# Differential attention: 768 columns scaled by ScalarE, and the products with the value in four portions of two key blocks

## What is computed

```python
sc = jnp.einsum('bqhmd,bkhmd->bmhqk', qb, k) * scale + bias[None, None]
p = jax.nn.softmax(sc, axis=-1)
a = p[:, 0] - lam * p[:, 1]
return jnp.einsum('bhqk,bkhd->bqhd', a.astype(v.dtype), v)
```

## Time and profile before

| | |
|---|---|
| median of 3 runs | 4118.57 us (4106.49 to 4128.41) |
| the profiled execution | 4106.46 us, of which its span 4104.7 us |
| busy over the span | PE 3779.6 us (92%), POOL 2494.2 (61%), DVE 2231.6 (54%), ACT 1659.1 (40%) |
| mean granted clock of PE | 0.979 of 2.4 GHz |

### The profile page before, as it was taken

The page is one execution under the profiler, slowest core; times in us unless marked ns, Lnnn a source line. Parts: engine busy times, 40 slices in busy tenths (PEclk is TensorE's granted clock), DMA queues, the critical chain, the costliest instruction groups (busy, mean ns, idle before and its releaser), DMA issues. The chain is left out here.

```text
span 4104.7 us, 51191 instructions
## 1 busy us (share of the span) xinstructions
PE 3779.6 (92%) x19002; PEld 2621.1 (64%) x19002; DVE 2231.6 (54%) x3655; ACT 1659.1 (40%) x2882; POOL 2494.2 (61%) x1393
## 2 busy tenths in 40 slices
PE   8999999999989999789989999999999898997898
PEld 8788774455545666557777897755455455665587
DVE  3012125555569999675531021255555699996754
ACT  3112104333348888661031121033333588886610
POOL 1221326877769999754512213277777699997555
PEclk9999999999999999999989999999999999999999
DMA  5333534232420222235354335322234202223353
GB/s 177 128 134 116 166 117 107 57 81 54 107 56 1 56 56 52 66 99 187 128 172 133 128 120 159 124 54 54 55 67 94 56 1 56 56 52 86 87 184 129
DMA packets 179678, 391.37 MB, mean 95 GB/s; under 512 B 17854, under 2 KB 98984, under 8 KB 167784
## 3 DMA queue, kind: packets, MB, share of 16 engines
q1 hardware_dynamic: 178568, 386.70, 33.6%
q10 hardware_dynamic: 864, 1.41, 0.2%
HBM read 254.88 MB, written 135.67 MB: 95 GB/s over the span
## 5 line engine op out<-in xcount | busy, mean ns | idle before, releaser
L1279 POOL TENSOR_TENSOR mla_sum_pool<-mla_sum_pool,mla_probs 128x1024 f32<-128x1024 f32 (+1 forms) x336 | 783.4, 2332 | 231.3 <-ACT mla_probs L1240 206.6
L1297 DVE TENSOR_REDUCE carry_row_max<-psum 128x1 f32<-128x512 f32 x688 | 473.4, 691 | 447.4 <-PE psum L1112 441.8
L1240 ACT ACTIVATE mla_probs<-psum 128x1024 f32<-128x1024 f32 x384 | 373.3, 1021 | 721.2 <-PE psum L1149 716.6
L1539 ACT ACTIVATE diff_probs<-psum,diff_shift 128x1024 f32<-128x1024 f32 x512 | 566.6, 1112 | 194.6 <-DVE diff_shift L1614 188.7
L1607 DVE TENSOR_REDUCE diff_row_max<-psum 128x1 f32<-128x1024 f32 x512 | 612.7, 1219 | 52.0 <-PE psum L1474 39.0
L1486 PE MATMUL psum<-ident,diff_probs 128*128 128x128 f32 x2048 | 329.4, 283 | 107.5 <-DVE diff_turned L1641 72.5
L624 PE MATMUL psum<-in_x_hi,in_w_hi 128*128 128x512 f32 x1024 | 403.1, 394 | 2.7 <-ACT in_mla_val L733 2.7
L624 PE MATMUL psum<-carry_firsts,in_w_hi 128*128 128x512 f32 x1024 | 403.4, 394 | 0.0
L624 PE MATMUL psum<-in_x_hi,in_w_lo 128*128 128x512 f32 x1024 | 400.3, 391 | 0.0
L1486 PEld LDWEIGHTS psum<-ident,diff_probs 128*128 128x128 f32 x2048 | 215.5, 141 | 286.0 <-issue 187.5
L1162 PE MATMUL psum<-mla_probs,mla_v_op 128*64 128x512 f32 x1536 | 373.2, 607 | 0.0
(11 more groups left out here) (206 smaller groups left out, 7383.9 us busy)
## 6 DMA issues: line engine op xcount, KB each, us to landing
in_w_raw<-in_w_in SPq DMA_DIRECT2D x64, 512.0 KB, 3.9
split_d<-in_out SPq DMA_DIRECT2D x64, 512.0 KB, 2.6
raw_d<-in_out SPq DMA_DIRECT2D x32, 512.0 KB, 2.6
mq_d<-in_out SPq DMA_DIRECT2D x48, 256.0 KB, 3.4
mk_d<-in_out SPq DMA_DIRECT2D x48, 256.0 KB, 3.9
carry_firsts<-split_d SPq DMA_DIRECT2D x48, 256.0 KB, 7.9
carry_weights<-split_d SPq DMA_DIRECT2D x48, 256.0 KB, 7.7
carry_weights<-split_d SPq DMA_DIRECT2D x16, 768.0 KB, 17.6
```

Source lines behind the costliest of these rows:

```text
L1240: nc.scalar.activation(probs[:, s % RING, :].rearrange("p (a n) -> p a n", n=CH), psum[:, S0 + 2 * (s % 2):S0 + 2 * (s % 2) + 2, :], ACT.E ...
L1279: nc.gpsimd.tensor_tensor(acc, start, probs[:, s % RING, mine], ALU.add).then_inc(pool_added, 1)
L1297: nc.vector.tensor_reduce(row_max[:, u % 2, qb, n:n + 1], psum[:, sweep_bank(g), :], AX.X, ALU.max).then_inc(maxed, 1)
L1539: nc.scalar.activation(dst[:, half * HALF:(half + 1) * HALF].rearrange("p (a n) -> p a n", n=CH), banks(n, m, half), ACT.Exp, bias=shift[: ...
```

## The change

Two things are changed in `diff_attention`, for both layers.

The split of the scaling: ACT's `scale` takes columns 0 to 767 instead of 0 to 511, and POOL's first instruction 768 to 1023 instead of 512 to 1023.

The order on PE: an iteration becomes four equal quarters of one half of scores, one batch of transposes, and one portion of products. A portion is two key blocks instead of four, there are four portions in an iteration instead of two, and each stands behind a batch of transposes instead of in front of one. The scores and the batches keep their order among themselves. What each portion waits for (`copied`, `o_ready`) names the same units as before. The queues of DVE, ACT and SP keep their order.

```diff
+    SCALED = 6 * P
...
-                    b, chunk = g // (NB // 2) % 2, 2 * ((n - 4) % 2) + place
-                    if chunk == 0 and g >= 1:
+                    b, first = g // (NB // 2) % 2, 8 * ((n - 4) % 2) + 2 * place
+                    if first == 0 and g >= 1:
                         pe.wait_ge(o_ready, g)
-                    pe.wait_ge(copied, 4 * (2 * g + 1) + chunk + 1)
-                    for kb in range(4 * chunk, 4 * chunk + 4):
+                    pe.wait_ge(copied, 4 * (2 * g + 1) + first // 4 + 1)
+                    for kb in range(first, first + 2):
...
-                    if chunk == 3:
+                    if first == NB - 2:
                         last.then_inc(pv_done, 1)
...
                 for n in range(UNITS + DRAIN + 2):
                     on = n < UNITS
-                    if on:
-                        scores(n, 0, 0)
-                    turns(n - LAG - 1, 3)
-                    if on:
-                        scores(n, 0, 1)
-                    products(n, 0)
-                    turns(n - LAG, 0)
-                    if on:
-                        scores(n, 1, 0)
-                    turns(n - LAG, 1)
-                    if on:
-                        scores(n, 1, 1)
-                    products(n, 1)
-                    turns(n - LAG, 2)
+                    for half in range(4):
+                        if on:
+                            scores(n, half // 2, half % 2)
+                        turns(n - LAG - (half == 0), (half - 1) % 4)
+                        products(n, half)
...
-                    first = probs1[:, n % DEEP1, 0:CH]
+                    first = probs1[:, n % DEEP1, 0:SCALED]
...
-                    second, third = probs1[:, n % DEEP1, CH:HALF], probs1[:, n % DEEP1, HALF:SEQ]
-                    nc.gpsimd.tensor_tensor(second, second, ratio[:, n % 2:n % 2 + 1].broadcast_to([P, HALF - CH]),
+                    second, third = probs1[:, n % DEEP1, SCALED:HALF], probs1[:, n % DEEP1, HALF:SEQ]
+                    nc.gpsimd.tensor_tensor(second, second, ratio[:, n % 2:n % 2 + 1].broadcast_to([P, HALF - SCALED]),
                                             ALU.mult).then_inc(times_ratio, 1)
```

## The result

| | before | after |
|---|---|---|
| median | 4116.33 us (4 runs, 4106.49 to 4128.41) | 4258.02 us (4 runs, 4244.85 to 4259.80) |
| ratio | | 1.0345, 95% interval 1.0327 to 1.0363 |
| span of the profiled execution | 4104.7 us | 4257.0 us |
| busy over the span | PE 3779.6, POOL 2494.2, DVE 2231.6, ACT 1659.1 | PE 3903.4, POOL 2438.1, DVE 2225.2, ACT 1686.5 |
| mean granted clock of PE | 0.979 | 0.976 |

The account below looks back on a forecast made before the run. POOL at 7.835 us a unit and a loop around PE were taken as nearly equal bounds. Portions lengthen units to 8.76 (upper) and 8.335 (lower), mean 8.55; 0.715 more over 120 units is 85.5 us, forecast 4204, range 4154 to 4240.

Parts of the forecast that it names:

- The two bounds on top of each other: In the differential stage, POOL at 7.835 us a unit and a loop around PE at 7.5 to 8.0.
- The cover: On PE, products lay where it waits for DVE's copy anyway; behind the batch, each portion adds 0.505 us to the loop.
- Each link between engines: In us: DVE's copy to batch 0.84, maximum to shift 1.26, shift to copy 0.18; ACT's loop 2.29, 2.20, 0.74.
- The odd half's wait: ACT's odd half waits for the last portion before map 1's exponential: 4.57 us, making an odd lower unit 8.60.
- rival 4: PE idles more and its clock falls from 2.4 to 1.2 GHz: some 690 us more, 4800, chance 0.01.
- rivals 1 to 3: POOL decides, 4065 us, chance 0.05; nothing moves, 4108, chance 0.08; only upper query blocks lose, 4174, chance 0.14.
- The products: On PE, 16 product instructions a unit as four portions of four, each taken as 0.505 us.
- the 0.39 for a batch: On PE, a batch of transposes takes 0.39 us before the next instructions start, in both loops.
- The upper bound of 0.58: On PE, a portion costs 0.42 us plus 0.16 if that excess belongs to the change of group.
- The upper blocks' idle time of PE in front of the batch: In each upper half unit, PE waits 0.7 us or more for DVE's copy, against 0.41 before.
- POOL's idle time: POOL's first instruction, never idle before, would wait for DVE's factor some 1.1 us a unit.

## Why the prediction was right and wrong

*Right.* The two bounds on top of each other, POOL at 7.835 and the loops around it: each alone relieved gave 1.0000 and 1.0005, both 0.9975. The cover: products were hidden under PE's wait for DVE's copy (left out, they bring 5 us) and are not hidden behind the batch. Each link between engines: 0.84, 1.26, 0.18, 2.20, 0.74, 2.29 forecast; 0.83, 1.26, 0.13, 2.19, 0.74, 2.27 measured. The odd half's wait, 32 of 32 groups. The clock: 1.00 in the stretch, so rival 4 fell, as did rivals 1 to 3. The ground given against rival 4 was weaker than it looked, though: the last 16 us of the stage had a granted clock of 0.99 with PE busy 7.85, but 0.50 with PE busy 7.13 when products were left out.

*Wrong.* The step "The products", and with it the 0.39 for a batch. I took a portion as half of 1.01, 0.505, and the batch in front of it at the 0.39 it took in front of scores. Measured are 0.58 and 0.56. With both terms corrected the sum of the prediction reads 8.55 + 2 x 0.245 = 9.04 a unit, less 7.835, times 120: 144.6 us, against 141.7 measured. The mean is right to this extent partly by luck: even units come out 0.14 too long that way and odd ones 0.1 too short, as the shorter links and the output's wait for ACT's odd half, neither of them in the forecast, nearly cancel. The end of the stage, which the forecast left as it was, is longer, too: from the last factor to the last output 18.7 us in the first layer, against 16.1 before.

Both prices could have been read. The upper bound of 0.58 for what follows a portion was exactly right. Yet I gave it half a voice, taking the middle of a fixed cost and no fixed cost, while the rows of eight in 1.01 and 32 in 3.67 already spoke for a fixed one. And I bounded the portion alone, and left out that it also changes what stands in front of it: at the stage's end the kernel before has products behind a batch, 0.56 later, and these are the 32 products from which I took the pace. The sum kept the 0.39 of another pair, batch and scores.

*Half right.* The upper blocks' idle time of PE in front of the batch, 0.7 or more forecast: it is 0.41 at 1408.17 and 0.38 at 1417.01, since the longer batches and portions fill a part of it, and 0.96 at 1422.07, behind DVE's output. POOL's idle time was put at the wrong one of its instructions; it waits for ACT's scale, which stands behind the exponentials of map 0 and a copy in ACT's queue. Two thirds of that wait, 68.3 of 102.0, is there with 512 columns as well.

## What to carry to other kernels

Before work is moved in a queue written by hand, find the wait that covers it and the loop that runs through its new place; the same instructions cost 5, 93 or 218 us here by place alone. An engine that is 97% full may still be worth nothing to relieve if a loop through others is as long: relieve both in one step, or the test of each alone says "no change" twice. A matmul group has a price at each change of kind that depends on its neighbours, so price the pairs, not the group. Look for the pair in the whole trace, the start and end of the stage included, where queues run in another pattern than inside the loop.

## What the runs showed of the hardware

- Products with a stationary operand of 64 columns, alternating between the two halves of the array, run in pairs: a pair of key blocks costs 0.43 us (portions of one and two pairs: 0.58 and 1.01 to the scores), and a portion of one block alone takes as long as one of a pair (0.57 to the scores, against 0.58). With 128 columns and the same count they don't pair: four instructions in 1.03 us against 0.65.
- Behind transposes the weights of a 64-column product are not loaded ahead: 0.56 us from the batch's start to the product's, in the changed kernel and at the stage's end in the kernel before, against 0.39 to scores and 0.47 to a 128-column product.
- With products left out, the granted clock of PE was 1.00 in a stretch in which it was busy 90.79 of 125 us. At the stage's end it was 0.77 from 1680 to 1700 us, with PE busy 12.04, and then 0.50 from 1700 to 1716 us, with 7.13 busy. The kernel before had 1.00 with 15.39 busy and 0.99 with 7.85 busy in the same two stretches.
